# State space input projection of a two-block layer as seven half-size products instead of eight, with three VectorE sums placed later

## The chip, the cores and the metric

The kernel runs on one core of one Trainium2 chip. The metric is the device time of one execution in microseconds (us), as the median of several runs. All data are float32. A core has a matrix engine (TensorE, PE in the profile, whose weight loads are listed as PEld), VectorE (DVE), ScalarE (ACT), GpSimd (POOL), and a queue engine (SyncE, SP) that issues most of the transfers from memory.

## The reference

256 tokens of width 1024 go through two blocks. The first is a hybrid of latent attention, gated linear attention and memory attention with a feed-forward part. The second is a state space branch beside dilated attention. The change touches the first projection of the second block, and the order of three sums elsewhere. Cut to that:

```
h = rms_norm_2(x, norm_w)
proj = h @ w_in                                # 256 x 1024 times 1024 x IN_WIDTH
u_s, z_s, q, k, v, z_a, r_s, r_a = split(proj) # u_s: 1024 columns
y_s = s5_branch(u_s, ...)                      # B u, a scan over time of 64 x 64 complex states, C h + D u,
                                               # gelu, glu
q = partial_rope(rms_norm_2(q)); k = partial_rope(rms_norm_2(k))
y_a = dilated_attention(q, k, v)
m = sigmoid(r_s) * (y_s * silu(z_s)) @ w_ssm_out + sigmoid(r_a) * (y_a * silu(z_a)) @ w_attn_out
x = x + m @ w_o
```

## The kernel before

The whole layer is one program without loops on the device. Each engine has its own instruction stream, in the order in which the source writes it, and semaphores join them. Nothing is reordered by a scheduler: what an engine has queued behind a wait waits with it.

Weights come through `ring`, three slots of 2 MB. SP issues the loads in the order of `JOBS` and waits before each (L512) until the job that used the slot last is finished. The two PSUM pairs of 1024 columns serve alternate outputs (`OUTS`), and an output may start only when the output two places ahead of it is taken out of its pair. Two `turned` banks hold transposes (and the state space outputs), two `score` banks hold scores (and the inputs of the states).

Most 1024 x 1024 projections are already "groups" (`group_multiply`, from L2073): rows and weights are cut in halves, and seven products of half the size in each dimension stand for eight. VectorE makes the sums of rows (`group_rows`: S1 to S4), the sums of weights (`group_t1` to `group_t4`), and puts the results together (`group_z`, `group_v`, `group_c12`, `group_c22`, `group_last`); ScalarE copies the products Q1 and Q5 out of PSUM (`group_copy`) and takes out the first block (`group_first`). Product 5 needs T1 and S1, 7 needs T3 and S3, 3 needs S4, 6 needs T2, 4 needs T4 and Z. T2 may only be made when product 5 is done, for both lie in one buffer.

The state space inputs `us0` and `us1` are not a group before the change. They are plain jobs, each by halves of tokens: `us0` on the first 128 tokens, the transposes of the second 128 tokens (`turn_rows("x", xn3, 1)`), then `us1` on the first tokens, and both on the second tokens. ScalarE takes them to `uT` (L844), and `stacks` copies `uT` to `u2`, half by VectorE (L1766, semaphore `u2_ready`) and half by ScalarE (L850).

Then the state space stage runs, eight rounds of m. In each TensorE makes `drive(m)` (the inputs of the states, L2479) and `states(m - 1)` (their outputs, L2460 to L2468), and fills the time with quarters of the jobs of `early`: dv0, dv1, dv2, zs0, zs1, za, dq0, dq1 (`fill`; a quarter is four matmuls of 512 columns, or eight of 256). VectorE scans the states and adds each output tile to `uT` (`ssm_out`). After `states(7)` VectorE runs `ssm_out(7)`, the argument of the gelu (`gelu_z`), and `dqk(0)`, the norm and rotation of the first queries. TensorE may turn those (`turn_dqk(0)`, L1987) only when `dqk(0)` is done (semaphore `dqk_rows`). Behind that it has the job dq2 and then `turn_dqk(1)`, which waits for `dqk(1)` in the same way.

Two other places matter. In the stage of memory attention, group `MV` (values of the memory) is followed by group `GT` (a gate), and a loop of i from 0 to 8 mixes them with scores and with levels of gated linear attention. In the dilated attention, a loop over s runs group `RA` between the scores.

Of the kernel before, what the change touches and what calls it, by code (L numbers as in the profile page):

```python
# [12 lines left out]
P = 128  # L13
# [70 lines left out]
DK = UP + 4  # L84
# [5 lines left out]
def jobs_table():  # L90
# [20 lines left out]
    j = [(f"us{i}", "w_in_2", C_US + 512 * i, 512) for i in range(2)]  # L111
    j += [(f"dv{g}", "w_in_2", C_DVV + DW * g, DW) for g in range(NDIL)]
# [17 lines left out]
ORDERS[GT] = ORDERS[UP] = ORDERS[WP] = (1, 2, 5, 7, 3, 6, 4)  # L130
# [3 lines left out]
ROWS = (0, 1, 1, 2, 3, 4) + 4 * (5,) + (6, 6, 6, 7, 8, 9)  # L134
# [4 lines left out]
BY_TOKENS = (("gate2", "gate3"), ("wo0", "wo1"), ("us0", "us1"))  # L139
HALVES = []  # L140
for _job in JOBS:
# [12 lines left out]
SPLIT_TOKENS = ("us0", "us1")  # L154
CHANNEL_MAJOR = {"ga", "us0", "us1", "zs0", "zs1", "za"}
# [49 lines left out]
    "u_ready": "state space inputs, even and odd steps stacked", "u2_ready": "first half of those stacks",  # L205
# [29 lines left out]
def act_at(i, n):  # L235

    return 3 * i + n - max(i - SO, 0) - (i > GT)
# [12 lines left out]
def build(nc, d, out):  # L250
    with ExitStack() as ctx:
# [133 lines left out]
        tail_t2 = {DK: arena[:, 0:2048], RS: arena[:, 2048:4096], RA: rows_raw, GLU: rows_raw, SO: arena[:, work_at:work_at + 2048], WP: arena[:, work_at + 4096:work_at + 6144]}  # L385
        tail_rows = {DK: m_tok, RS: m_tok, RA: m_tok, GLU: zs, SO: arena[:, work_at + 2048:work_at + 4096], WP: rows_raw}

# [24 lines left out]
        def group(i):  # L412
# [3 lines left out]
            w = [ring[:, STREAMED.index(JOB[f"g{i}{x}"]) % RING, :].rearrange("p (k n) -> p k n", n=DM) for x in "xy"]  # L416
            b11, b12, b21, b22 = (x[:, :, 512 * n:512 * n + 512] for x in w for n in range(2))
            if i < DK:
# [12 lines left out]
        def temporaries(i):  # L431
            if i >= DK:
                return tail_q1, tail_q5, tail_q5, tail_q1
            if i == MV:
                return copied_q1, across, across, copied_q1
            if i == GT:
# [34 lines left out]
        def _(sp):  # L471
# [21 lines left out]
            for n, j in enumerate(STREAMED):  # L493
# [9 lines left out]
                if n >= RING:  # L503

                    before = JOBS[STREAMED[n - RING]][0]
                    if before[:-1] in GROUPS:
# [59 lines left out]
        def _(act):  # L566
# [12 lines left out]
            def take(name, dst, func=ACT.Copy, scale=1.0, cols=512):  # L579

                for t in range(TT):
                    p = arrived(name, 1 if name in SPLIT_TOKENS else t)
# [54 lines left out]
            def group_first(i, dst, scale=1.0):  # L637
# [5 lines left out]
                act.activation(dst, src, ACT.Relu if UP <= i < DK else ACT.Copy, scale=scale).then_inc(sem("group_act"), 1)  # L643
# [197 lines left out]
            for i in range(2):  # L841
                for t in range(TT):
                    p = arrived(f"us{i}")
                    ins = act.activation(uT[:, 1024 * i + 512 * t:1024 * i + 512 * t + 512], p[:, 512 * t:512 * t + 512], ACT.Copy)  # L844
# [99 lines left out]
        def _(dve):  # L944
# [83 lines left out]
            def group_t1(i):  # L1028

                _, _, (b11, b12, _, _), _, (t2, _) = group(i)  # L1030
                weights_in(f"g{i}x")
                if i == GT:
# [305 lines left out]
            group_rows(GT)  # L1338
# [48 lines left out]
            group_middle(MV, vm4[1], vm4[3])  # L1387
            level_diff(0)
            gt4 = by_tokens(gate_buf)
            h, (_, _, z, v), biased = group(GT)[0], temporaries(GT), ckv[:, 0:512]  # L1390
            for i in range(9):
                if i == 0:
                    group_t1(GT)
                if i == 1:
# [70 lines left out]
                if i in (4, 6):  # L1465
                    gate_gain((i - 4) // 2)
# [256 lines left out]
            turns_real(64, high)  # L1723
            turns_imag(64, high)

# [123 lines left out]
            for s in range(DH // 2 + 1):  # L1849
                if s == 2:  # L1850
                    group_c12(RA, ra4[1])
                if s < DH // 2:
# [6 lines left out]
                    if s == 0:  # L1859
                        group_t3(RA)  # L1860
# [108 lines left out]
        def _(pe):  # L1969
# [25 lines left out]
            def matmuls(name, half):  # L1995
# [17 lines left out]
                if o in SPLIT_TOKENS:  # L2013
                    return [(p[:, SEQ * c + P * half:SEQ * c + P * half + P], ws[:, k, P * c:P * c + P],
                             act_(k)[:, P * half:P * half + P], k == 0, k == nk - 1) for c in range(4) for k in range(nk)]
# [10 lines left out]
            def half_job(name, half, sub=0, of=1):  # L2026
# [3 lines left out]
                if half == 0 and sub == 0:  # L2030
# [4 lines left out]
                    if i >= 2 and FIRST_JOB[o] == name:  # L2035
# [37 lines left out]
            def group_multiply(i, q, channels=False, sub=0, of=1):  # L2073
# [18 lines left out]
                bank_, rows, weights = {1: (1, a11, b11), 5: (3, s1, t2), 2: (1, a12, b21), 7: (4, s3, t3), 3: (3, s4, b22),  # L2092
# [7 lines left out]
                elif q == 5:  # L2100
                    summed(1)
                    rows_summed(1)
                elif q == 2:
# [15 lines left out]
                onto = q in (2, 3, 4)  # L2119
# [368 lines left out]
            pe.wait_ge(sem("ca_ready"), 2)  # L2488
            for m in range(8):
# [185 lines left out]
```

## Time and profile before

| | |
|---|---|
| median of 3 runs | 966.28 us (965.92 to 966.91) |
| the profiled execution's own time | 964.69 us |
| its span in the profile | 962.8 us |
| TensorE busy | 947.7 us, 98% |
| VectorE busy | 719.3 us, 75% |
| ScalarE busy | 224.1 us, 23% |
| chain that ended last, by engine | PE 89%, DVE 8%, ACT 2% |
| share of 16 DMA engines, queue of the weights | 39.8% |

TensorE is busy nearly always, so the time is its work plus its few waits. A float32 matmul of the source stands as two MATMUL records in the trace, so "x64" there is 32 matmuls. The mean duration of a record is longer than the distance between two starts, because matmuls are pipelined: the pace is read from the start of one group of records to the start of the next. The 1.9 us between the span and the execution's own time lie outside the program.

### The profile page before, as it was taken

Reading aid. Unit: us, or ns where it says so; the run is one execution under the profiler, and the core shown is the slowest. Engines: PE = TensorE matmul, PEld = TensorE weight load, DVE = VectorE, ACT = ScalarE, POOL = GpSimd, SP = SyncE. Lnnn points to the kernel's source line nnn. Section 1 sums busy time; section 2 is a strip of 40 time slices with the busy share of each in tenths; the row PEclk is TensorE's granted clock in tenths of the full one; section 3 lists DMA queues with packets and bytes.
Section 4 is the critical chain, followed back from the end, with each engine's and each line's share of the span. In section 5 each row is a group of like instructions: output and inputs, shape, how many; then the busy total and the mean of one; then the engine's idle time right before and its main releaser. Section 6 shows DMA issues by size and latency. Waiting matters only on the chain.

```text
span 962.8 us, 12510 instructions
## 1 busy us (share of the span) xinstructions
PE 947.7 (98%) x4998; PEld 587.7 (61%) x4998; DVE 719.3 (75%) x1260; ACT 224.1 (23%) x442; POOL 23.3 (2%) x27
## 2 busy tenths in 40 slices
PE   7999999999999999999999999999999999999998
PEld 6944445754555449999844459447854444468544
DVE  4875964578968887966899863988968689674667
ACT  4313412223231223422200011201012221434100
POOL 0100000000002500000000000000000000000000
PEclk9999999999999999999999999999999999999999
DMA  9551731434534524344444433523424443321631
GB/s 329 151 197 43 285 131 44 175 117 147 165 120 124 174 107 167 131 176 175 175 175 174 174 122 142 175 88 113 151 88 175 161 143 142 113 97 45 223 127 45
DMA packets 51770, 139.76 MB, mean 145 GB/s; under 512 B 3968, under 2 KB 7904, under 8 KB 51712
## 3 DMA queue, kind: packets, MB, share of 16 engines
q1 hardware_dynamic: 50256, 135.07, 39.8%
q0 software_dynamic: 1248, 3.80, 1.6%
q8 instruction: 40, 0.66, 0.3%
q14 instruction: 18, 0.15, 0.0%
q10 hardware_dynamic: 208, 0.08, 0.0%
HBM read 137.90 MB, written 1.05 MB: 144 GB/s over the span
## 4 chain that ended last, share of the span: by engine, by line
PE 89%; DVE 8%; ACT 2%; issue 1%; DMA 1%; DVEq 0%; ACTq 0%
PE pair L2042 30%; PE pair L2127 22%; PE pair L2123 16%; PE pair L2384 6%; DVE arena L974 4%; PE turned L1987 4%; PE score L2384 3%; PE turned L2384 1%; PE score L2479 1%; PE score L2551 1%; PE score L2564 1%; PE score L2226 1%; PE score L2225 1%; PE score L2281 1%; DMA ident<-in_c_ident 1%
## 5 line engine op out<-in xcount | busy, mean ns | idle before, releaser
L2042 PE MATMUL pair<-ring,hT 128*128 128x512 f32 (+2 forms) x512 | 213.6, 572 | 0.9 <-ACT hT L622 0.9
L974 DVE TENSOR_TENSOR arena<-arena 128x256 f32<-128x256 f32 (+6 forms) x332 | 196.7, 607 | 17.2 <-PE score L2384 4.0
L2042 PEld LDWEIGHTS pair<-ring,hT 128*128 128x128 f32 x512 | 95.3, 190 | 102.6 <-issue 97.7
L2127 PE MATMUL pair<-ring,arena 128*128 128x512 f32 x192 | 85.8, 594 | 0.0
L2127 PE MATMUL pair<-ring,hT 128*128 128x512 f32 x184 | 84.0, 598 | 1.3 <-DMA ring<-in_w_in 0.7
L2127 PE MATMUL pair<-arena 128*128 128x512 f32 x176 | 79.8, 595 | 0.4 <-DVE arena L974 0.4
L974 DVE TENSOR_TENSOR arena<-pair,arena 128x512 f32<-128x512 f32 x60 | 41.5, 692 | 49.6 <-PE pair L2127 25.6
L2042 PE MATMUL pair<-hT,ring 128*128 128x128 f32 (+2 forms) x464 | 76.2, 324 | 0.2 <-ACT hT L622 0.2
L974 DVE TENSOR_TENSOR arena<-ring 128x2048 f32<-128x2048 f32 (+1 forms) x39 | 72.3, 1855 | 2.5 <-DMA ring<-in_w_ssm_out 1.2
L2042 PEld LDWEIGHTS pair<-hT,ring 128*128 128x128 f32 (+1 forms) x464 | 66.0, 188 | 8.6 <-ACT hT L622 1.0
L2123 PE MATMUL pair<-arena 128*128 128x128 f32 x544 | 64.0, 276 | 0.0
L2123 PEld LDWEIGHTS pair<-arena 128*128 128x128 f32 x544 | 62.2, 192 | 0.3 <-issue 0.2
L2127 PEld LDWEIGHTS pair<-ring,arena 128*128 128x128 f32 x192 | 35.6, 190 | 41.4 <-issue 41.3
L2127 PEld LDWEIGHTS pair<-ring,hT 128*128 128x128 f32 x184 | 33.4, 190 | 39.5 <-issue 38.4
L2127 PEld LDWEIGHTS pair<-arena 128*128 128x128 f32 x176 | 32.8, 190 | 39.3 <-issue 38.4
L2123 PE MATMUL pair<-hT,ring 128*128 128x128 f32 x480 | 55.7, 275 | 0.0
L2123 PEld LDWEIGHTS pair<-hT,ring 128*128 128x128 f32 x480 | 54.7, 192 | 0.7 <-issue 0.5
L1987 PEld LDWEIGHTS turned<-ident,arena 128*128 128x128 f32 (+1 forms) x363 | 41.1, 141 | 22.7 <-issue 16.5
L593 ACT ACTIVATE arena<-turned 128x512 f32<-128x512 f32 (+2 forms) x66 | 32.8, 540 | 87.5 <-PE turned L1987 87.5
L1987 PE MATMUL turned<-ident,arena 128*128 128x128 f32 (+1 forms) x363 | 49.9, 275 | 2.2 <-DVE arena L1876 0.9
L974 DVE TENSOR_TENSOR arena<-arena,ring 128x2048 f32<-128x2048 f32 (+1 forms) x24 | 46.5, 1937 | 1.7 <-PE pair L2123 0.6
L2384 PE MATMUL pair<-ring,arena 128*128 128x512 f32 x96 | 43.5, 592 | 0.0
(226 smaller groups left out, 1009.3 us busy)
## 6 DMA issues: line engine op xcount, KB each, us to landing
ring<-in_w_in SPq DMA_DIRECT2D x33, 2048.0 KB, 8.4
ring<-in_w_up SPq DMA_DIRECT2D x8, 2048.0 KB, 8.6
ring<-in_w_down SPq DMA_DIRECT2D x8, 2048.0 KB, 7.9
ring<-in_w_o SPq DMA_DIRECT2D x4, 2048.0 KB, 8.0
ring<-in_w_mem_kv SPq DMA_DIRECT2D x2, 2048.0 KB, 7.7
ring<-in_w_glu SPq DMA_DIRECT2D x2, 2048.0 KB, 8.1
ring<-in_w_ssm_out SPq DMA_DIRECT2D x2, 2048.0 KB, 7.8
ring<-in_w_ukv SPq DMA_DIRECT2D x4, 512.0 KB, 3.7
```

Of the source, the lines that this page charges most:

```text
L593: act.activation(dst, src, ACT.Copy).then_inc(sem("turned_taken"), 1)
L974: return dve.tensor_tensor(o, a, b, op)
L1987: ins = pe.transpose(b[0:x.shape[1], a:a + rows], x, ident[0:rows, 0:rows])
L2042: ins = pe.matmul(o_, s, m, start=a, stop=b)
L2123: ins = pe.matmul(h[bank_][:, P * c:P * c + P], weights[:, k, P * c:P * c + P], rows[:, k, :], start=not onto and c == 0 and k == 0, stop= ...
L2127: ins = pe.matmul(h[bank_], rows[:, k, :], weights[:, k, :], start=not onto and k == 0, stop=k == 3, skip_group_check=True)
L2225: pe.matmul(o, qnT[:, SEQ * h + P * t:SEQ * h + P * t + P], knT[:, SEQ * h:SEQ * h + w], start=True, stop=False)
L2226: ins = pe.matmul(o, qpT[r, SEQ * (h // 2) + P * t:SEQ * (h // 2) + P * t + P], kpeT[r, 0:w], start=False, stop=True)
L2281: ins = pe.matmul(b[:, SEQ * t:SEQ * t + SEQ], s[:, 256 * t + P * k:256 * t + P * k + P], vm3[:, k, EV * h:EV * h + EV], start=k == 0, sto ...
L2384: ins = pe.matmul(product[q], rows[:, k, :], weights[:, k, :], start=g == 0 and k == 0, stop=g == 7 and k == 1, skip_group_check=True)
L2479: ins = pe.matmul(b[:, 256 * h + P * i:256 * h + P * i + P], bt[r, 2048 * i + P * n:2048 * i + P * n + P], u2[r, CH * n:CH * n + CH], star ...
L2551: ins = pe.matmul(b[:, cols], qdT[r, a + P * t:a + P * t + P], kdT[r, a:a + w], start=True, stop=True)
```

## The change

`us0` and `us1` become the group `US`, number 10, and the groups behind it move up by one. Its weights are split by columns and not by rows: the first load holds columns 512 to 1023 of all 1024 rows, so products 1 and 2 need that load alone. Product 2 has a PSUM bank of its own (half 2 of the second pair) and is added to Q1 by VectorE. Products 1 and 2 take the place of `us0` on the first tokens; after the transposes comes the first half of `dv0`, which had been in `early`, and then products 5, 7, 3, 6, 4. `early` starts three quarters later, and each round takes its quarters from three places on. VectorE makes the sums in its stream around `turns_real` and `turns_imag(64, high)`. ScalarE copies Q1 and Q5 instead of four blocks.

Apart from it, `group_rows(GT)` moves behind `group_middle(MV, ...)`, the two `gate_gain` move from the ends of i = 4 and 6 to the starts of i = 4 and 5, `group_t3(RA)` moves behind the first heads of s = 0, and `group_t4(RA)` from s = 0 to s = 1.

```diff
-    j = [(f"us{i}", "w_in_2", C_US + 512 * i, 512) for i in range(2)]
-    j += [(f"dv{g}", "w_in_2", C_DVV + DW * g, DW) for g in range(NDIL)]
+    out += [(f"g{US}{'xy'[i]}", f"g{US}{'ab'[i]}", "w_in_2", 0, DM, C_US + 512 * (1 - i), 512) for i in range(2)]
+    j = [(f"dv{g}", "w_in_2", C_DVV + DW * g, DW) for g in range(NDIL)]
...
+                    if before[:-1] == f"g{US}":
+                        sp.wait_ge(sem("group_product"), product_at(US, 4 if before[-1] == "x" else 6))
...
-            for i in range(2):
-                for t in range(TT):
-                    p = arrived(f"us{i}")
-                    ins = act.activation(uT[...], p[:, 512 * t:512 * t + 512], ACT.Copy)
-                    if t == 0:
-                        ins.then_inc(sem("u_ready"), 1)
-                ins.then_inc(sem("taken_act"), 1)
-            act.wait_ge(sem("taken_act"), taken("us1")[1])
+            group_copy(US, 1)
+            group_copy(US, 5)
+            act.wait_ge(sem("last_out"), US + 1)
             for h, jj, s, src, dst in stacks(1):
...
-            group_rows(GT)
...
             group_middle(MV, vm4[1], vm4[3])
+            group_rows(GT)
             level_diff(0)
...
+                if i in (4, 5):
+                    gate_gain(i - 4)
...
-                if i in (4, 6):
-                    gate_gain((i - 4) // 2)
...
             turns_real(64, high)
+            group_t1(US)
+            dve.wait_ge(sem("turned_taken"), T_B + 4)
+            group_rows(US)
+            us4 = by_channels(uT)
+            h, (q1, _, _, v) = group(US)[0], temporaries(US)
+            dve.wait_ge(sem("group_product"), product_at(US, 2))
+            dve.wait_ge(sem("group_act"), act_at(US, 1))
+            link(tt(us4[1], blocks(h[2], us4[1]), blocks(q1, us4[1]), ALU.add))
+            group_t3(US)
             turns_imag(64, high)
+            group_t2(US)
+            group_t4(US)
+            group_z(US)
+            group_v(US)
+            dve.wait_ge(sem("group_product"), product_at(US, 3))
+            mark(tt(us4[0], blocks(h[3], us4[0]), blocks(v, us4[0]), ALU.add), "first_out")
+            group_c22(US, us4[2])
...
-            dve.wait_ge(sem("taken_act"), taken("us0")[1])
             for h, jj, s, src, dst in stacks(0):
...
+            group_last(US, us4[3])
...
-                    if s == 0:
-                        group_t3(RA)
...
                 if s == 0:
+                    group_t3(RA)
                     group_t2(RA)
+                if s == 1:
                     group_t4(RA)
-                if s == 1:
...
-            half_job("us0", 0)
+            group_multiply(US, 1, True)
+            group_multiply(US, 2, True)
             pe.wait_ge(sem("x_rows"), 6)
             turn_rows("x", xn3, 1)
-            half_job("us1", 0)
+            pe.wait_ge(sem("group_act"), act_at(US, 1))
+            half_job("dv0", 0, own_wait=True)
             is_turned("x")
-            half_job("us0", 1)
-            half_job("us1", 1)
+            for q in (5, 7, 3, 6, 4):
+                group_multiply(US, q, True)
+            pe.wait_ge(sem("first_out"), US + 1)
...
+            fill(early, 2, 1)
             for m in range(8):
...
                 drive(m)
-                fill(early, 3 * m, 1)
-                fill(early, 3 * m + 1, 1)
+                fill(early, 3 * m + 3, 1)
+                fill(early, 3 * m + 4, 1)
                 if m:
                     states(m - 1)
-                fill(early, 3 * m + 2, 1)
-            fill(early, 12, 2)
+                fill(early, 3 * m + 5, 1)
+            fill(early, 27, 1)
+            fill(early, 28, 1)
             states(7)
-            fill(early, 13, 2)
-            fill(early, 14, 2)
+            fill(early, 29, 1)
             fill(early, 15, 2)
```

The order on TensorE around the projection, before: the first rows are the end of the feed-forward's last products and the transposes of the first tokens; `pair<-hT,ring` is `us0` and `us1`, `pair<-ring,hT` is dv0, `score<-arena` is `drive`.

```order
L2384 MATMUL score<-arena 128x512 x2
L2042 MATMUL pair<-hT,ring 128x128 x32
L1987 MATMUL turned<-ident,arena 128x128 x8
L2042 MATMUL pair<-hT,ring 128x128 x96
L2479 MATMUL score<-arena 128x128 x8
L2042 MATMUL pair<-ring,hT 128x512 x12
```

The same place of the changed kernel: products 1 and 2, the transposes, half of dv0, products 5, 7 and 3, 6, 4, and a quarter of dv0.

```order
L2403 MATMUL score<-arena 128x512 x2
L2142 MATMUL pair<-hT,ring 128x128 x32
L2006 MATMUL turned<-ident,arena 128x128 x8
L2058 MATMUL pair<-ring,hT 128x512 x8
L2142 MATMUL pair<-arena 128x128 x16
L2142 MATMUL pair<-arena,ring 128x128 x32
L2142 MATMUL pair<-arena 128x128 x16
L2142 MATMUL pair<-hT,ring 128x128 x16
L2058 MATMUL pair<-ring,hT 128x512 x4
L2501 MATMUL score<-arena 128x128 x8
```

128 matmuls of 128 columns have become 112, and 12 of the 512-column matmuls now stand ahead of the first `drive`.

TensorE at the end of the state space stage, before: the last `drive`, quarters of dq0, `states(6)`, more of dq0, `states(7)` (the second set of `turned<-arena`), the rest of dq0 and dq1, then `turn_dqk(0)` (`turned<-ident,arena`) and the job dq2.

```order
L2466 MATMUL turned<-arena 32x128 x8
L2460 MATMUL turned<-arena 32x128 x4
L2468 MATMUL turned<-arena 32x127 x8
L2042 MATMUL pair<-ring,hT 128x512 x24
L1987 MATMUL turned<-ident,arena 128x128 x8
L2042 MATMUL pair<-ring,hT 128x512 x16
```

The same place of the changed kernel.

```order
L2488 MATMUL turned<-arena 32x128 x8
L2482 MATMUL turned<-arena 32x128 x4
L2490 MATMUL turned<-arena 32x127 x8
L2058 MATMUL pair<-ring,hT 128x512 x12
L2006 MATMUL turned<-ident,arena 128x128 x8
L2058 MATMUL pair<-ring,hT 128x512 x16
```

Between the last state outputs and the transposes of the queries stand 12 matmuls of 512 columns instead of 24.

## Rows read from the trace of the kernel before

**Rows 1.** The page: TensorE's busy time, and its granted clock in 40 slices.
```profile
PE 947.7 (98%) x4998; PEld 587.7 (61%) x4998; DVE 719.3 (75%) x1260; ACT 224.1 (23%) x442; POOL 23.3 (2%) x27
...
PEclk9999999999999999999999999999999999999999
```

**Rows 2.** Timeline of TensorE, projection: start, us, engine, line, operation, records [idle before].
```profile
571.28 7.41 PE L2042 MATMUL pair<-hT,ring 128*128 128x128 f32 x64 [0.17 <-ACT hT L622]
578.53 1.04 PE L1987 MATMUL turned<-ident,arena 128*128 128x128 f32 x8
579.40 21.60 PE L2042 MATMUL pair<-hT,ring 128*128 128x128 f32 x192
600.93 1.16 PE L2479 MATMUL score<-arena 64*128 64x128 f32 x16
602.03 10.57 PE L2042 MATMUL pair<-ring,hT 128*128 128x512 f32 x24
```

**Rows 3.** Timeline of ScalarE, same place.
```profile
579.23 2.17 ACT L622 ACTIVATE hT<-turned,pcol 128x128 f32<-128x128 f32 x8 [6.13 <-PE turned L1987]
...
609.20 0.60 ACT L583 ACTIVATE arena<-pair 128x512 f32<-128x512 f32 x1 [1.62 <-PE pair L2042]
```

**Rows 4.** Loads by SP's line 512, from 568 to 572 us: issues, and time to landing.
```profile
L512 SPq DMA_DIRECT2D ring<-in_w_in x2: 368/368/368, 568.5 to 571.1; - x2
...
DMA to landing us min/median/max: 8.3/9.6/11.0
```

**Rows 5.** The same from 100 to 104 us.
```profile
L512 SPq DMA_DIRECT2D ring<-in_w_in x2: 368/368/368, 100.1 to 103.5; - x2
...
DMA to landing us min/median/max: 8.4/9.8/11.1
```

**Rows 6.** Timeline of VectorE, projection.
```profile
576.12 7.28 DVE L974 TENSOR_TENSOR arena<-arena 128x1024 f32<-128x1024 f32 x6
595.08 3.57 DVE L1766 COPY arena<-arena 32x512 f32<-32x512 f32 x8 [11.69 <-ACT arena L844]
```

**Rows 7.** Timeline of VectorE, end of the state space stage and first queries.
```profile
714.37 0.48 DVE L1774 SCALAR_TENSOR_TENSOR arena<-arena,pcol,turned 128x256 f32<-128x256 f32 x1 [5.02 <-PE turned L2468]
...
723.58 1.22 DVE L1737 TENSOR_REDUCE stats<-arena 128x16 f32<-128x1024 f32 x1 [2.24 <-ACT arena L886]
...
730.58 0.62 DVE L974 TENSOR_TENSOR arena<-arena 128x128 f32<-128x128 f32 x2
731.24 1.42 DVE L974 TENSOR_TENSOR arena<-hT 128x512 f32<-128x512 f32 x2
...
734.14 5.00 DVE L974 TENSOR_TENSOR arena<-arena 128x1024 f32<-128x1024 f32 x4
...
746.84 2.29 DVE L974 TENSOR_TENSOR arena<-ring 128x2048 f32<-128x2048 f32 x1
```

**Rows 8.** Timeline of TensorE, same place.
```profile
714.16 20.87 PE L2042 MATMUL pair<-ring,hT 128*128 128x512 f32 x48
734.87 1.04 PE L1987 MATMUL turned<-ident,arena 128*128 128x128 f32 x8
...
749.48 1.04 PE L1987 MATMUL turned<-ident,arena 128*128 128x128 f32 x8
```

**Rows 9.** Timeline of TensorE, first product of group GT.
```profile
224.69 3.67 PE L2127 MATMUL pair<-ring,hT 128*128 128x512 f32 x8 [0.58 <-DVE arena L974]
```

**Rows 10.** Timelines of VectorE and then TensorE, end of the loop over i.
```profile
293.28 1.23 DVE L974 TENSOR_TENSOR arena<-arena,gains 128x1024 f32<-128x1024 f32 x1
...
300.26 1.56 PE L2308 MATMUL score<-arena 128*128 128x256 f32 x6 [0.82 <-DVE arena L1425]
```

**Rows 11.** Timeline of TensorE, dilated attention.
```profile
826.76 0.87 PE L1987 MATMUL turned<-ident,arena 128*128 128x128 f32 x6 [0.92 <-DVE arena L1876]
...
835.77 0.70 PE L2551 MATMUL score<-arena 64*128 64x256 f32 x4 [0.41 <-DVE stats L1254]
```

**Rows 12.** Timeline of TensorE, its first matmuls.
```profile
5.63 3.96 PE L2134 MATMUL score<-ident 128*128 128x128 f32 x20 [5.63 <-DMA ident<-in_c_ident]
```

More of the change, by code:

```diff
@@ L83 @@
 RG, MV, GT, UP = 3, 4, 5, 6
-DK = UP + 4
+US = UP + 4
+DK = US + 1
 RS = DK + 1
@@ L129 @@
 ORDERS = {i: (1, 5, 2, 7, 3, 6, 4) for i in range(NG)}
-ORDERS[GT] = ORDERS[UP] = ORDERS[WP] = (1, 2, 5, 7, 3, 6, 4)
+ORDERS[GT] = ORDERS[US] = ORDERS[UP] = ORDERS[WP] = (1, 2, 5, 7, 3, 6, 4)
 ORDERS[RA] = (1, 5, 2, 7, 6, 3, 4)
-ROWS = (0, 1, 1, 2, 3, 4) + 4 * (5,) + (6, 6, 6, 7, 8, 9)
+ROWS = (0, 1, 1, 2, 3, 4) + 4 * (5,) + (6, 7, 7, 7, 8, 9, 10)
 LAST_JOB = {job[1]: job[0] for job in JOBS}
 FIRST_JOB = {job[1]: job[0] for job in reversed(JOBS)}
-BY_TOKENS = (("gate2", "gate3"), ("wo0", "wo1"), ("us0", "us1"))
+BY_TOKENS = (("gate2", "gate3"), ("wo0", "wo1"))
 HALVES = []
@@ L152 @@
 BY_DVE = {"gg", "wo0", "wo1", "ao0", "ao1"} | {f"gate{i}" for i in range(2, 6)}
-SPLIT_TOKENS = ("us0", "us1")
-CHANNEL_MAJOR = {"ga", "us0", "us1", "zs0", "zs1", "za"}
+CHANNEL_MAJOR = {"ga", "zs0", "zs1", "za"}
 STREAMED = [n for n, job in enumerate(JOBS) if job[2]]
@@ L204 @@
     "m0_ready": "TensorE: B times C, by group", "m0_taken": "that product out of PSUM",
-    "u_ready": "state space inputs, even and odd steps stacked", "u2_ready": "first half of those stacks",
+    "u2_ready": "first half of those stacks",
     "u2_late": "ScalarE: their second half",
@@ L415, in group @@
             h = {1: a[:, 0:512], 3: a[:, 512:1024], 2: b[:, 0:512], 4: b[:, 512:1024]}
-            w = [ring[:, STREAMED.index(JOB[f"g{i}{x}"]) % RING, :].rearrange("p (k n) -> p k n", n=DM) for x in "xy"]
-            b11, b12, b21, b22 = (x[:, :, 512 * n:512 * n + 512] for x in w for n in range(2))
-            if i < DK:
+            w = [ring[:, STREAMED.index(JOB[f"g{i}{x}"]) % RING, :].rearrange("p (k n) -> p k n", n=512 if i == US else DM) for x in "xy"]
+            if i == US:
+                b11, b12, b21, b22 = (x[:, 4 * n:4 * n + 4, :] for n in range(2) for x in w)
+            else:
+                b11, b12, b21, b22 = (x[:, :, 512 * n:512 * n + 512] for x in w for n in range(2))
+            if i < US:
                 t2, t3 = (x.rearrange("p (k n) -> p k n", n=512) for x in ((sum_t2[i], sum_t3) if i < UP else (up_t2, up_t3)))
@@ L505, in _ @@
                     before = JOBS[STREAMED[n - RING]][0]
-                    if before[:-1] in GROUPS:
+                    if before[:-1] == f"g{US}":
+                        sp.wait_ge(sem("group_product"), product_at(US, 4 if before[-1] == "x" else 6))
+                    elif before[:-1] in GROUPS:
                         sp.wait_ge(sem("group_product"), product_at(GROUPS.index(before[:-1]), 7 if before[-1] == "x" else 4))
@@ L1031, in group_t1 @@
                 weights_in(f"g{i}x")
+                if i == US:
+                    weights_in(f"g{i}y")
                 if i == GT:
@@ L2024, in _, with half_job @@
             finished = [0]
-            def half_job(name, half, sub=0, of=1):
+            def half_job(name, half, sub=0, of=1, own_wait=False):
                 j = JOB[name]
@@ L2034, in half_job @@
                     i = OUTS.index(o)
-                    if i >= 2 and FIRST_JOB[o] == name:
+                    if i >= 2 and FIRST_JOB[o] == name and not own_wait:
                         by, v = taken(OUTS[i - 2])
@@ L2090, in free @@
                     pe.wait_ge(sem(by), v)
-                bank_, rows, weights = {1: (1, a11, b11), 5: (3, s1, t2), 2: (1, a12, b21), 7: (4, s3, t3), 3: (3, s4, b22),
+                bank_, rows, weights = {1: (1, a11, b11), 5: (3, s1, t2), 2: (2 if i == US else 1, a12, b21), 7: (4, s3, t3), 3: (3, s4, b22),
                                         6: (2, s2, t2), 4: (4, a22, b21)}[q]
@@ L2100, in group_multiply @@
                 elif q == 5:
+                    came(f"g{i}{'y' if i == US else 'x'}")
                     summed(1)
                     rows_summed(1)
+                elif q == 2 and i == US:
+                    free(OUTS[b - 2])
                 elif q == 2:
@@ L2118, in group_multiply @@
                     pe.wait_ge(sem("group_z"), i + 1)
-                onto = q in (2, 3, 4)
+                onto = q in (3, 4) or q == 2 and i != US
                 if channels:
```

16 lines of the change are left out of this document (7 added, 9 removed).

## The prediction

> **What bounds the kernel now.** I read the page first: TensorE is busy 98% of the span at the full granted clock in all 40 slices [rows 1]. So the time is TensorE's stream, and an edit counts only by the work that it takes out of that stream and by the waits that it opens or closes there. VectorE has a quarter of its time free, but its order decides when TensorE may go on. Next I read the timelines of TensorE, ScalarE, VectorE and the loads around the projection, and then followed TensorE's stream to the places at which it meets VectorE again.
>
> In the projection TensorE has no wait after 571.28 [rows 2]: from there it runs 163.59 us without one, up to the first queries' transposes at 734.87 [rows 2, 8]. VectorE meanwhile stands still for 11.69 us ahead of its copies [rows 6]. The other waits of TensorE that the change can reach are 0.58 [rows 9], 0.82 [rows 10], 0.92 and 0.41 [rows 11].
>
> **The work saved.** 192 records take 600.93 - 579.40 = 21.53 us, 0.112 each and 0.224 for a matmul of the source [rows 2]. The group has 7 x 16 = 112 of them where there were 128: 16 x 0.224 = **-3.6 us**.
>
> **First wait: Q1 has to be copied.** Products 1 and 2 take as long as `us0` on the first tokens, so the transposes start at 578.53 as before and end their issue at 579.40 [rows 2]. Then stood `us1`, which could run while ScalarE took the transposes out. Now TensorE waits for `group_copy(US, 1)`, because dv0 goes into the bank of Q1. ScalarE has the copy queued behind eight evictions that wait for the very transposes: 579.23 + 2.17 = 581.40, and a copy of 512 columns takes 0.60 [rows 3], so 582.05. The weights of dv0 are issued at 571.1 and land 11.0 later, at 582.1 [rows 4], the same moment. Cost: 582.1 - 579.4 = **+2.7 us** (bounds 2.5 and 3.0). That half of dv0 does not come free: it fills the time of VectorE's sums, but begins only behind this wait.
>
> **The sums, hidden.** `turns_real` ends half way in 7.28 us, at 579.8 [rows 6]. A sum of weights takes 2.29, four sums of rows 734.14 - 731.24 = 2.9 [rows 7]. T1 is ready at 582.1, the rows at 585.0, us4[1] at 585.7, T3 at 588.0, `turns_imag` at 591.7. TensorE's half of dv0 (eight matmuls; 48 records in 20.71 us are 0.863 for each matmul [rows 8]) ends at 589.1, so products 5 and 7 find their sums. Product 5 ends at 592.7, T2 at 595.2, T4 at 597.6, both ahead of products 6 (599.9) and 4 (603.5). `first_out` comes at 605.2, ahead of TensorE's 607.1. The copies of 3.57 us [rows 6] make `u2_ready` at 609.5; TensorE has a quarter of dv0 until 610.6. The 15 us that VectorE has to add lie in the time in which it stood still; this cover has 1.1 us left, and beyond that each us would be TensorE's.
>
> **A load that starts later.** dv1 uses the slot of the group's first load, and SP waits for product 4, so it is issued at 607.2, behind all of the group. A load takes 8.3 to 8.4 when one follows closely, for the second waits and not the first (8.3 beside 11.0, 8.4 beside 11.1) [rows 4, 5]. So dv1 lands at 615.6. TensorE wants it after `drive(0)` (1.1 [rows 2]) and one quarter (3.5), at 615.1. Cost: **+0.5 us** (bounds 0, and 5 if two loads issued 0.4 us apart shared the rate from the start; the trace's closest neighbours are 2.7 us apart, and I take the lower price).
>
> **Second wait: the first queries come too late.** This is the term that decides. `drive(0)` starts 3 quarters later in the job list, so every round of the state space stage stands 10.4 us deeper in TensorE's work, `states(7)` too. Behind it were 24 matmuls, 20.71 us [rows 8]; now 12, 10.4 us. What VectorE must do between `states(7)` and `turn_dqk(0)` is unchanged, and it is a chain: it starts at 714.37, waiting 5.02 for the output [rows 7]; `ssm_out(7)` and the gelu's argument end at 723.58 - 2.24 = 721.34; `dqk(0)` runs from 723.58 to 731.20 [rows 7]. Without the 2.24 us of waiting for dq0, which is now complete earlier, the chain is 6.97 + 0.04 + 7.62 = 14.6 us, and 14.9 from the moment 0.2 ahead at which TensorE leaves `states(7)`, wake-up included. TensorE had 20.7 us to hide it in and keeps 10.4: 14.9 - 10.4 = **+4.5 us** of waiting at the transposes (bounds 4.0 and 5.0).
>
> **The second queries.** From the end of `dqk(0)` to that of `dqk(1)` VectorE needs 746.8 - 731.2 = 15.6 us [rows 7]; TensorE needs 749.48 - 734.87 = 14.6 between the two transposes [rows 8]. VectorE was 749.48 - 746.8 = 2.7 us ahead; after the second wait both start together, so **+1.0 us** more. For the third, `dqk(2)` starts as soon as dq2 is squared, 7.6 us of chain beside 14.6 us of TensorE: it has room, and the stream is back in its old order.
>
> **The three sums.** `group_rows(GT)`, 2.9 us, stood ahead of the block for which the 0.58 us wait was [rows 9]; behind the change VectorE starts that block as soon as MV's product 6 is there. The wait goes; but VectorE itself gets on no earlier, and TensorE meets it again later in the loop: **-0.4 us** (bounds -0.6 and 0). `gate_gain`, 1.23 us, stood ahead of the level whose later copies hold TensorE 0.82 us [rows 10]; at the starts of i = 4 and 5 VectorE is idle. Part of it was hidden by the wait for a score: **-0.4 us** (bounds -0.8 and 0). `group_t3(RA)` and `group_t4(RA)`, 2.29 each [rows 7], leave the ways to the 0.92 and the 0.41 us wait [rows 11]: some 0.9 us at first. But T4 now lies in s = 1 ahead of `group_t1(GLU)`, and pushes VectorE's first scores of s = 2 back by about 1.1 us, where TensorE waits for both score banks. I take **0** (bounds -0.9 and +0.4), for the delay is as long as the gain.
>
> **The sum.** -3.6 + 2.7 + 0.5 + 4.5 + 1.0 - 0.4 - 0.4 + 0 = +4.3 us. The profiled execution took 964.69 us, 1.9 more than its span, and would take 969.0; the median of the runs is 1.6 above it, 966.28, and becomes **970.6 us**. The lead of half a projection costs more at its end than the eighth product gives.
>
> **Rivals.** (a) Not slower: the queries' chain still fits. It decides at the point where TensorE's work behind `states(7)` reaches 14.9 us; if the outputs came a quarter and more earlier, or the gelu's argument ran ahead, 5.5 us of the sum go and 970.6 becomes 965.1. For it: VectorE waits 5.02 us for those outputs, so it could start earlier if TensorE gave them. Against: TensorE's order is fixed, and 12 matmuls stand there. Chance 0.12.
> (b) The full gain: neither the copy of Q1 nor the queries stop TensorE; -3.6 and about -1 from the sums, 961.7. It needs two of my chains wrong, so 0.05.
> (c) A slower clock after the longest wait. No stretch of the trace shows less than the full clock, 2.4 GHz, in its slices [rows 1], but after the 5.63 us in which TensorE stood still at the start its first 20 records took 3.96 us, 0.198 each [rows 12], against 0.112 later [rows 2]: 1.7 us for such a start. A wait of 4.5 us is nearly as long. 1.0 us of it would vanish in the wait for the second queries, so 971.3; after both waits 973. Chance 0.15. The Trainium skill, "TensorE: Matmul & The Clock Gate", section "Why this matters for your kernels", says that idle gaps between bursts of matmuls bring the engine back to half its clock; by that the dearer end of this rival would hold, and only the slow first records speak for it here.
> (d) The two loads share the rate, dv1 lands 4 to 5 us later: 975. Against it is the pattern of rows 4 and 5. Chance 0.05.
>
> **How the numbers follow.** The forecast itself has 0.63; 970.6 with its own bounds of 969.3 to 972. The range reaches down past the bounds of the small terms and toward (a), and up over (c): 967.0 to 973.4. About 0.2% (1.9 us) is what a measurement of this kernel can tell from no change. Slower by more: the forecast, (c), (d) and a slip of the terms, 0.82. Within: (a), 0.11. Faster by more: (b) and part of (a), 0.07.
>
> **What would show each step.** In the changed profile TensorE's busy time falls by about 3.6 us and its idle time rises by about 8. One idle of some 2.5 us stands ahead of dv0's first matmul, put down to ScalarE's copy or the load; one of some 4.4 ahead of the first queries' transposes and one of 1 ahead of the second, both put down to VectorE's rotation; one of up to 0.5 at dv1's first quarter. VectorE no longer waits 2.24 us for the squares of dq0. The 0.58 us at GT is gone. If the transposes of the queries show no wait, the central term is wrong; if `drive(0)` waits for VectorE's copies, the cover of the sums was thinner than I reckoned; if the matmuls behind the long wait run at 0.2 us a record, it is (c).

## The result: half a per cent slower, and the profile after

The changed kernel takes 971.12 us (970.37 to 972.92, 4 runs) where the kernel before takes 966.47 us: a ratio of 1.0055, 95% interval 1.0043 to 1.0067. The quotient of the two medians is 1.0048, inside that interval, so the loss is 4.7 to 5.3 us. Run again later the changed kernel took 970.84 us, 1.0055 (1.0043 to 1.0068). The forecast was 970.6 us. One execution of the first experiment below (1406.62 us, mean granted clock 0.655) and one of the second (1230.17 us, 0.754) are in the medians given there, but not in the ratios.

The page after, as its first lines and its granted clock:

```profile
span 968.4 us, 12476 instructions
...
PE 947.7 (98%) x4966; PEld 585.6 (60%) x4966; DVE 735.3 (76%) x1274; ACT 223.5 (23%) x440; POOL 23.4 (2%) x27
...
PEclk9999999999999999999999999999999999999999
```

The span is 5.6 us longer. TensorE has 32 records fewer than in [rows 1] (16 matmuls of the source) and yet the same busy time, 947.7 us. That is a first sign that some of its records have become slower. VectorE has 16 us more work, the sums of the new group.

The timeline of TensorE in the projection, which answers to [rows 2]:

```profile
569.98 7.41 PE L2142 MATMUL pair<-hT,ring 128*128 128x128 f32 x64 [0.17 <-ACT hT L629]
577.23 1.04 PE L2006 MATMUL turned<-ident,arena 128*128 128x128 f32 x8
580.73 8.80 PE L2058 MATMUL pair<-ring,hT 128*128 128x512 f32 x16 [2.47 <-ACT arena L642]
589.37 3.73 PE L2142 MATMUL pair<-arena 128*128 128x128 f32 x32
...
610.76 1.16 PE L2501 MATMUL score<-arena 64*128 64x128 f32 x16
```

Products 1 and 2 take the place of `us0`. Then TensorE stands idle for 2.47 us until ScalarE's line 642, the copy of Q1, is done. The half of dv0 behind it takes 589.37 - 580.73 = 8.64 us, where 8 matmuls at 0.863 would be 6.90. From there all products follow without a wait: the sums are hidden.

ScalarE and the two loads at the same place, as in [rows 3, 4]:

```profile
577.92 2.18 ACT L629 ACTIVATE hT<-turned,pcol 128x128 f32<-128x128 f32 x8 [6.13 <-PE turned L2006]
579.94 0.65 ACT L642 ACTIVATE arena<-pair 128x512 f32<-128x512 f32 x1
...
L519 SPq DMA_DIRECT2D ring<-in_w_in x2: 368/368/368, 567.2 to 569.8; - x2
...
DMA to landing us min/median/max: 8.1/9.4/10.8
```

The copy ends at 580.6, and the load of dv0's weights lands at 569.8 + 10.8 = 580.6.

The two loads behind the group, dv1's first, with the shortest and the longest time to landing. Asked for alone, the one issued at 607.4 lands after 7.9 us:

```profile
L519 SPq DMA_DIRECT2D ring<-in_w_in x2: 368/476/583, 607.4 to 607.8; - x2
...
DMA to landing us min/median/max: 7.9/10.4/12.9
```

TensorE at the end of the state space stage, as in [rows 8], and VectorE, as in [rows 7]:

```profile
724.10 10.57 PE L2058 MATMUL pair<-ring,hT 128*128 128x512 f32 x24
739.05 1.94 PE L2006 MATMUL turned<-ident,arena 128*128 128x128 f32 x8 [4.38 <-issue]
740.78 14.51 PE L2058 MATMUL pair<-ring,hT 128*128 128x512 f32 x32
755.12 1.04 PE L2006 MATMUL turned<-ident,arena 128*128 128x128 f32 x8
...
724.31 0.48 DVE L1794 SCALAR_TENSOR_TENSOR arena<-arena,pcol,turned 128x256 f32<-128x256 f32 x1 [7.32 <-PE turned L2490]
...
731.32 1.22 DVE L1757 TENSOR_REDUCE stats<-arena 128x16 f32<-128x1024 f32 x1
...
738.32 0.62 DVE L976 TENSOR_TENSOR arena<-arena 128x128 f32<-128x128 f32 x2
...
753.93 0.62 DVE L976 TENSOR_TENSOR arena<-arena 128x128 f32<-128x128 f32 x2
```

VectorE begins behind `states(7)` at 724.31 and ends the rotation of the first queries at 738.94. TensorE is through with its 12 matmuls at 734.5 and starts the transposes at 739.05. The profile names no releaser for those 4.38 us ("issue"); the end of the rotation 0.1 us ahead of them does. A label is no proof, so the runs below test it.

Behind both waits the granted clock fell. The stretches of the changed kernel (columns: stretch, its length, then busy us and records of PE, PEld, DVE, ACT, POOL, then the granted clock as a share of 2.4 GHz, the share of the DMA engines, GB/s):

```profile
575.00:580.00 5.00, 3.26 (x30) 3.02 (x28) 4.93 (x4) 2.08 (x9) 0.00 (x0) 1.00 0.98 364
580.00:585.00 5.00, 4.27 (x6) 1.82 (x7) 4.80 (x7) 0.59 (x2) 0.00 (x0) 0.66 0.02 6
...
735.00:740.00 5.00, 0.95 (x5) 0.98 (x6) 4.79 (x10) 1.77 (x4) 0.00 (x0) 0.86 0.84 296
740.00:745.00 5.00, 5.00 (x14) 2.77 (x13) 4.83 (x6) 1.20 (x2) 0.00 (x0) 0.80 0.31 125
```

A share of 0.66 or 0.80 over 5 us is a part of that time at the lower level, 1.2 GHz. Read in steps of 1 us, the clock is still at its full level when TensorE works again behind the first wait (1.00 from 580 to 581), and at 0.50 from 582 to 584. At the second it falls while TensorE still stands idle (0.79 from 738 to 739) and is at 0.50 from 739 to 742. The forty slices of the page are too coarse to show it.

Where the 5.6 us lie, from TensorE's marks in the two traces (each step is the distance between two starts, after less before; the three quarters of dv0 that stand elsewhere are counted out at 10.36 us):

| stretch of TensorE | after less before, us |
|---|---|
| start to the end of the last transposes of MV (216.44 for 217.07) | -0.63; the wait for the first load was 4.9 for 5.63 us |
| to the projection (569.98 for 571.28) | -0.67 |
| to the first `drive` (40.78 - 10.36 for 29.65) | +0.77 = -3.6 + 2.6 + 1.7 |
| to the end of `states(7)` (113.34 for 113.23) | +0.11 |
| to the first queries' transposes (14.95 for 20.71 - 10.36) | +4.60 |
| to the second queries' transposes (16.07 for 14.61) | +1.46 |
| to the end of the span | -0.04 |
| sum | +5.60 |

### The profile page after: what moved, and what is told of

It reads as the page before. It is cut to its first block, busy times and chain, and to the rows that moved or that the text cites. A ratio compares the mean times of both kernels' runs of the same rounds, so it can differ in the third digit from the quotient of the medians.

```text
span 968.4 us, 12476 instructions
## 1 busy us (share of the span) xinstructions
PE 947.7 (98%) x4966; PEld 585.6 (60%) x4966; DVE 735.3 (76%) x1274; ACT 223.5 (23%) x440; POOL 23.4 (2%) x27
## 4 chain that ended last, share of the span: by engine, by line
PE 86%; DVE 10%; ACT 2%; issue 1%; DMA 0%; DVEq 0%; ACTq 0%
PE pair L2058 28%; PE pair L2146 20%; PE pair L2142 18%; DVE arena L976 6%; PE pair L2403 6%; PE turned L2006 3%; PE score L2403 3%; PE turned L2403 1%; PE score L2574 1%; PE score L2501 1%; PE score L2245 1%; DVE ring L976 1%; PE score L2244 1%; PE score L2587 1%; ACT hT L629 1%
## 5 line engine op out<-in xcount | busy, mean ns | idle before, releaser
L2058 PE MATMUL pair<-ring,hT 128*128 128x512 f32 (+2 forms) x512 | 216.3, 577 | 3.3 <-ACT arena L642 2.5
L976 DVE TENSOR_TENSOR arena<-arena 128x256 f32<-128x256 f32 (+6 forms) x333 | 197.4, 607 | 14.9 <-PE score L2403 4.1
L976 DVE TENSOR_TENSOR arena<-pair,arena 128x512 f32<-128x512 f32 x64 | 44.3, 692 | 55.3 <-PE pair L2146 25.8
L2146 PE MATMUL pair<-ring,arena 128*128 128x512 f32 x192 | 85.8, 594 | 0.0
L2142 PE MATMUL pair<-arena 128*128 128x128 f32 x608 | 71.5, 275 | 0.0
L2142 PEld LDWEIGHTS pair<-arena 128*128 128x128 f32 x608 | 69.6, 192 | 0.7 <-issue 0.7
L2142 PE MATMUL pair<-hT,ring 128*128 128x128 f32 x576 | 66.8, 275 | 0.2 <-ACT hT L629 0.2
L2142 PEld LDWEIGHTS pair<-hT,ring 128*128 128x128 f32 x576 | 65.6, 192 | 1.7 <-ACT hT L629 1.0
L2146 PEld LDWEIGHTS pair<-arena 128*128 128x128 f32 x176 | 32.8, 190 | 39.3 <-issue 38.4
L2058 PE MATMUL pair<-hT,ring 128*128 128x256 f32 (+1 forms) x208 | 47.2, 383 | 0.0
L2142 PE MATMUL pair<-arena,ring 128*128 128x128 f32 x384 | 46.0, 277 | 0.0
L2142 PEld LDWEIGHTS pair<-arena,ring 128*128 128x128 f32 x384 | 44.0, 192 | 1.3 <-issue 1.0
```

Of the source, the lines that this page charges most:

```text
L976: return dve.tensor_tensor(o, a, b, op)
L2058: ins = pe.matmul(o_, s, m, start=a, stop=b)
L2142: ins = pe.matmul(h[bank_][:, P * c:P * c + P], weights[:, k, P * c:P * c + P], rows[:, k, :], start=not onto and c == 0 and k == 0, stop= ...
L2146: ins = pe.matmul(h[bank_], rows[:, k, :], weights[:, k, :], start=not onto and k == 0, stop=k == 3, skip_group_check=True)
```

## Experiments

**The state outputs earlier.** If VectorE's chain behind `states(7)` is what TensorE waits for, giving it five quarters to hide in and not three has to remove both waits at the queries.

```diff
-            fill(early, 27, 1)
-            fill(early, 28, 1)
             states(7)
+            fill(early, 27, 1)
+            fill(early, 28, 1)
             fill(early, 29, 1)
```

> The changed kernel with one edit: states(7) stands directly behind the last round, so that 20 matmuls of 512 columns (17.3 us) and not 12 (10.4 us) lie between the last state outputs and the first queries' transposes. Theory (VectorE's chain of 14.9 us behind states(7) is what TensorE waits for): the waits of 4.4 us and of about 1 us ahead of the first and second queries go, and with them the slow clock behind the first of them; 971.1 - 4.6 - 1.5 = 965.0 us. Rival (ScalarE's squares or evictions, or the TensorE stream itself, set those transposes): the wait stays, 970 to 971 us. Second rival: states(7) now waits for VectorE's scan of round 7, which ends only some 0.4 us ahead of it; then a new wait of up to 1 us stands there, 966 us.

Measured: 965.22 us, 0.9993 of the kernel before (0.9984 to 1.0002), so 6.0 us below the changed kernel. TensorE at that place:

```profile
714.89 0.65 PE L2488 MATMUL turned<-arena 128*32 128x128 f32 x16
...
716.40 17.43 PE L2058 MATMUL pair<-ring,hT 128*128 128x512 f32 x40
733.67 1.04 PE L2006 MATMUL turned<-ident,arena 128*128 128x128 f32 x8
734.54 13.90 PE L2058 MATMUL pair<-ring,hT 128*128 128x512 f32 x32
748.28 1.04 PE L2006 MATMUL turned<-ident,arena 128*128 128x128 f32 x8
```

No wait stands there any more, and no slow transposes. `states(7)` itself does not wait for the scan. The position of the last outputs in TensorE's stream alone made the loss at the queries. It is the main one: mended, the change is level with the kernel before. The first wait is still there, 2.39 us long.

**The copy first.** The first wait has two ends that coincide, the copy and the load. Taking one away tells whether the other holds.

```diff
             for t in range(TT):
                 act.wait_ge(sem("residual"), 2 * TT + 2 * t + 2)
                 row_norm(t, xres[:, t, :], 0, "x", uT[:, 0:1024])
+                if t == 1:
+                    group_copy(US, 1)
                 turned_rows(t, hT, "norm_w_2")
-            group_copy(US, 1)
             group_copy(US, 5)
```

> The changed kernel with one edit: ScalarE copies Q1 ahead of the eight evictions of the second tokens' transposes. Theory (the copy and the load of dv0's weights end at the same moment, 580.6 us): TensorE waits as long as before, now for the load; 970.9 us, gain at most 0.2 us. Rival (only the copy holds TensorE): the wait of 2.5 us and the slow clock behind it go, 967.0 us.

Measured: 971.27 us, 1.0053 (1.0040 to 1.0066): no gain. ScalarE's copy and TensorE's first dv0 record:

```profile
574.60 0.60 ACT L642 ACTIVATE arena<-pair 128x512 f32<-128x512 f32 x1 [2.11 <-issue]
...
581.61 8.80 PE L2059 MATMUL pair<-ring,hT 128*128 128x512 f32 x16 [2.65 <-DMA ring<-in_w_in]
```

The copy is done at 575.2, more than 6 us earlier relative to the work around it, and TensorE waits 2.65 us all the same, now for the load. An edit at ScalarE alone, where the profile's releaser pointed, gains nothing. (The profiled execution, 974.38 us, was the longest of the five in the ratio.) The load alone holds TensorE; whether the copy alone would hold it as long was not run.

**Kept busy.** Is the slow clock caused by TensorE's own idling, and what does it cost? Extra matmuls fill the waits without shortening them.

```diff
+            pe.wait_ge(sem("residual"), 8)
+            for _n in range(10):
+                pe.matmul(bank["score"][0][:, 0:P], ident[:, :], ident[:, :], start=True, stop=True)
             pe.wait_ge(sem("group_act"), act_at(US, 1))
             half_job("dv0", 0, own_wait=True)
...
+            pe.wait_ge(sem("score_taken"), n_unit["score"])
+            for _n in range(18):
+                pe.matmul(bank["score"][0][:, 0:P], ident[:, :], ident[:, :], start=True, stop=True)
             pe.wait_ge(sem("ssm_taken"), 8)
```

> The changed kernel with matmuls of the identity in the two long waits (10 of 128 columns ahead of dv0, 18 ahead of the first queries' transposes), written to a score bank that nobody reads then. They are extra work and do not shorten the waits. Theory (the slow stretches behind the waits, 1.7 us at dv0 and 1.5 us at the queries of which about 1 would be waited out anyway, come from TensorE's idling): 971.1 - 1.7 - 0.5 = 968.9 us, and the granted clock stays at its full level. Rival (the slow stretches have nothing to do with the idling): 971.1 us or a little more.

Measured: 968.82 us, 1.0036 (1.0024 to 1.0048), 1.9 thousandths or 1.8 us below the changed kernel, with more work in it.

```profile
581.09 7.11 PE L2058 MATMUL pair<-ring,hT 128*128 128x512 f32 x16 [0.44 <-DMA ring<-in_w_in]
...
733.25 4.18 PE L2540 MATMUL score<-ident 128*128 128x128 f32 x36
737.79 1.06 PE L2006 MATMUL turned<-ident,arena 128*128 128x128 f32 x8 [0.36 <-issue]
...
753.34 1.09 PE L2006 MATMUL turned<-ident,arena 128*128 128x128 f32 x8 [0.75 <-DVE arena L976]
...
735.00:740.00 5.00, 4.64 (x34) 3.76 (x34) 4.76 (x11) 1.60 (x4) 0.00 (x0) 1.00 1.00 396
```

The granted clock stays at its full level, with a mean of 1.000 in each of the five executions, where all nine executions of the changed kernel had 0.996. The half of dv0 takes 7.1 us again and the transposes 1.06 where they took 1.94. The wait for the second queries, which the slow clock had covered in the changed kernel, comes to light: 0.75 us of idle, 737.79 to 753.34 being 15.55 where 14.61 is the work alone.

**The three sums alone**, on the kernel before (the projection is left as it was; the edit is that of the change, at GT, the gains and RA).

> The kernel before with the three moved sums alone (rows of GT, the two gains, T3 and T4 of RA); the projection stays as it was. Theory: GT's wait goes and the one at the end of the loop is halved, RA gives 0.9 us and takes it back; -0.7 us, 965.8 us. Rival (the dilated attention's gain is real and only the state space part costs): -1.6 us, 964.9 us. Rival on the other side: a wait for VectorE elsewhere takes it all back, 966.5 us.

Measured: 964.50 us, 0.9989 (0.9981 to 0.9998), 1.0 us faster, with an interval that nearly reaches 1. It holds both the -0.7 us of the theory and the -1.6 us of the first rival; only the trace tells them apart. TensorE:

```profile
224.41 3.60 PE L2126 MATMUL pair<-ring,hT 128*128 128x512 f32 x8
...
250.50 0.70 PE L2296 MATMUL score<-arena 128*32 128x32 f32 x32 [0.51 <-DVE stats L1254]
...
300.08 1.56 PE L2307 MATMUL score<-arena 128*128 128x256 f32 x6 [0.45 <-DVE arena L1427]
...
826.12 0.87 PE L1986 MATMUL turned<-ident,arena 128*128 128x128 f32 x6 [0.45 <-DVE arena L1874]
...
853.29 0.70 PE L2550 MATMUL score<-arena 64*128 64x256 f32 x4 [0.85 <-DVE stats L1254]
```

GT's wait of [rows 9] is gone, but a new one of 0.51 us stands 26 us later: TensorE, ahead now, meets VectorE's scores. The wait of [rows 10] is halved. In the dilated attention both waits of [rows 11] shrink, 0.92 to 0.45 and 0.41 to nothing, and 0.85 us come back in the scores of s = 2, as the theory had it.

**Without the lead.** The lead undone: no dv0 in the projection, the rounds and the place of `states(7)` as before.

```diff
-            pe.wait_ge(sem("group_act"), act_at(US, 1))
-            half_job("dv0", 0, own_wait=True)
             is_turned("x")
...
-            fill(early, 2, 1)
...
-                fill(early, 3 * m + 3, 1)
-                fill(early, 3 * m + 4, 1)
+                fill(early, 3 * m, 1)
+                fill(early, 3 * m + 1, 1)
...
-                fill(early, 3 * m + 5, 1)
-            fill(early, 27, 1)
-            fill(early, 28, 1)
+                fill(early, 3 * m + 2, 1)
+            fill(early, 12, 2)
             states(7)
-            fill(early, 29, 1)
+            fill(early, 13, 2)
+            fill(early, 14, 2)
```

> The changed kernel without the lead: no half of dv0 between the transposes and product 5, no quarter of it ahead of the first drive, and the quarters of the rounds and the place of states(7) as in the kernel before. Theory: TensorE now waits for VectorE's sums, about 3.5 us ahead of product 5, 1.6 ahead of product 7 and 2.3 ahead of the first drive, while 24 matmuls hide the queries' chain again. Against the kernel before +3.9 us in the projection (the saved 3.6 included) and -0.7 from the three sums: 969.7 us, up to 971 with a slow clock. Rival (the sums are ready anyway and the lead was not needed): 962 us. Rival (the queries' wait does not come from the lead): 974 us or more.

Measured: 969.35 us, 1.0041 (1.0027 to 1.0055), 3.4 us over the kernel before.

```profile
582.33 5.44 PE L2142 MATMUL pair<-arena 128*128 128x128 f32 x32 [3.36 <-DVE arena L976]
...
604.68 1.16 PE L2499 MATMUL score<-arena 64*128 64x128 f32 x16 [2.62 <-DVE arena L1785]
...
717.91 20.87 PE L2058 MATMUL pair<-ring,hT 128*128 128x512 f32 x48
738.62 1.04 PE L2006 MATMUL turned<-ident,arena 128*128 128x128 f32 x8
```

Now TensorE waits for the sums, 3.36 us ahead of product 5 and 2.62 ahead of the first `drive`, and the wait of 1.6 us that I expected ahead of product 7 vanished, because product 5 ran slowly (5.27 us for 3.57) in the meantime. At the queries there is no wait. So the lead does what it is for, and the lead is what opens the wait 130 us later. Neither with it nor without it does the group pay in this form.

**Both mended.** The two waits attacked at once, by order alone.

```diff
             group_multiply(US, 1, True)
-            group_multiply(US, 2, True)
+            group_multiply(US, 2, True, 0, 2)
             pe.wait_ge(sem("x_rows"), 6)
             turn_rows("x", xn3, 1)
+            group_multiply(US, 2, True, 1, 2)
+            is_turned("x")
+            group_multiply(US, 5, True)
             pe.wait_ge(sem("group_act"), act_at(US, 1))
             half_job("dv0", 0, own_wait=True)
-            is_turned("x")
-            for q in (5, 7, 3, 6, 4):
+            for q in (7, 3, 6, 4):
...
-            turns_real(64, high)
             group_t1(US)
...
             group_t3(US)
+            turns_real(64, high)
             turns_imag(64, high)
```

with ScalarE's copy as in the second experiment and `states(7)` as in the first.

> The changed kernel with both waits attacked. ScalarE copies Q1 ahead of the evictions; the transposes stand in the middle of product 2; product 5 stands ahead of dv0's half and covers the rest of its load; VectorE makes T1, the rows, us4[1] and T3 ahead of turns_real; states(7) stands behind the last round. Theory: about 1.1 us of waiting is left ahead of product 5, too short for a slow clock, so -3.3 us in the projection and -6.1 us at the queries: 961.9 us, below both kernels. Rival (the sums now come late for products 7, 6 or the first drive, whose cover was 1.2 us): 963 to 965 us.

Measured: 962.74 us, 0.9969 (0.9958 to 0.9980), and 962.19 us, 0.9966 (0.9952 to 0.9979) when it was run again: 3.2 us faster than the kernel before.

> The kernel of e6 again, as the measure for e7 on the same chip: 0.9969 of the kernel before.

```profile
580.85 3.81 PE L2144 MATMUL pair<-arena 128*128 128x128 f32 x32 [0.93 <-DVE arena L978]
584.49 7.03 PE L2060 MATMUL pair<-ring,hT 128*128 128x512 f32 x16
...
609.18 1.16 PE L2505 MATMUL score<-arena 64*128 64x128 f32 x16
```

A wait of 0.93 us is left, for S1, and the clock stays up. Products 7 and 6 and the first `drive` do not wait, so the rival's late sums are not there. The two places gave what was expected of them: from the projection to the first `drive` TensorE takes 37.55 us for 40.78 (-3.2), and from the end of `states(7)` to the second queries 31.88 us for 31.02, with 8 matmuls more in it, 6.9 us (-6.0). The profiled execution lost 1.65 us ahead of the projection (571.63 for 569.98), where the edit changes nothing.

**T1 of GLU later.** The last 0.85 us.

```diff
                     group_c22(RA, ra4[3])
-                    group_t1(GLU)
...
+                    if s == 2:
+                        group_t1(GLU)
                     for e in range(2):
                         h = 2 * s + e
```

> The kernel of e6 with one edit more: T1 of GLU (2.29 us on VectorE) moves from s = 1 into the idle time of VectorE between the second and the third scores of s = 2. Theory (T4 of RA and T1 of GLU together push VectorE's first scores of s = 2 back, and TensorE waits 0.85 us for the score banks): that wait goes and the 0.9 us gained earlier stay; 0.85 us below e6 on the same chip, 0.9991 of it. Rival (the third scores, now up to 0.5 us later, pass their delay on to the transposes, whose room was 1.9 us): no gain.

Measured: 961.09 us, 0.9954 (0.9941 to 0.9966), beside 0.9966 of the kernel without this edit on the same chip: 1.1 us less, a difference that the two intervals by themselves do not separate. The trace shows its place: the scores that waited 0.85 us follow at once. From the matmuls ahead of them to the end of the span it takes 111.41 us, beside 112.08 in the trace of the kernel without the edit: by the traces 0.67 of the 1.1 us are its doing.

```profile
847.39 1.98 PE L2149 MATMUL pair<-ring,hT 128*128 128x512 f32 x4
849.30 0.70 PE L2579 MATMUL score<-arena 64*128 64x256 f32 x4
```

This is the fastest version, 4.9 us below the kernel before.

**The changed kernel again.**

> The changed kernel itself, on the chip of e6 and e7: 1.0055 of the kernel before. If the slow clock behind its two waits does not come in every execution, its runs spread over some 3 us and wider than the kernel before's; if it is always there, they spread as those do.

Measured: 970.84 us (970.46 to 971.52, 5 runs). Its stretches, columns as above:

```profile
580.00:585.00 5.00, 3.56 (x9) 1.68 (x10) 4.83 (x6) 1.35 (x5) 0.00 (x0) 1.00 0.12 40
...
735.00:740.00 5.00, 1.98 (x9) 2.01 (x10) 4.76 (x11) 1.35 (x4) 0.00 (x0) 0.65 0.95 373
740.00:745.00 5.00, 5.00 (x9) 1.98 (x9) 4.83 (x6) 0.59 (x1) 0.00 (x0) 0.67 0.09 37
```

TensorE in the same trace, at the half of dv0 and at the transposes of the first and second queries:

```profile
581.44 7.10 PE L2058 MATMUL pair<-ring,hT 128*128 128x512 f32 x16 [2.41 <-ACT arena L642]
...
738.02 1.94 PE L2006 MATMUL turned<-ident,arena 128*128 128x128 f32 x8 [4.37 <-issue]
...
755.27 1.04 PE L2006 MATMUL turned<-ident,arena 128*128 128x128 f32 x8
```

In this execution the clock did not fall behind the first wait. Behind the second it was low for longer: 0.65 and 0.67 for 0.86 and 0.80, and the second transposes follow after 755.27 - 738.02 = 17.25 us, not 16.07. So 1.7 us were saved at one place and 1.2 paid at the other. That fits the five times, which lie within 1.1 us where the expectation had some 3 us. The mean granted clock, which is known of every execution, tells how often it falls: 0.996 in all nine of the changed kernel, and never under 0.999 in the 43 of the kernel before that stand beside the experiments. In the first experiment, where only the first wait is left, it is 0.998 in five of the ten executions in the ratio and 1.000 in the other five. Why it falls behind that wait in some executions and not in others stays open.

## Why the prediction was right, point by point

The time (971.12 for 970.6), the sign and the main mechanism came out as forecast, by these steps.

- *The work saved*, 3.6 us: right. It is hard to see in the page, because slowed records filled TensorE's busy time up again; my own sign for it, a busy time lower by 3.6 us, did not appear, and the idle time rose by 5.6 us and not by 8.
- *First wait*, 2.7 us: 2.63 by the starts. That copy and load end together was right: both are at 580.6 in the trace, and in the second experiment, the copy gone, the wait stays at 2.65.
- *The sums, hidden*: right, at every product. The first `drive` found its copies made 1.1 us ahead (VectorE ended them at 609.66, TensorE came at 610.76).
- *The later load*, +0.5: 0.11. The first of two loads issued 0.4 us apart landed in 7.9 us, not 8.4, while the second took 12.9. Rival (d), sharing, was wrong.
- *Second wait*, 4.5 us: 4.60. The chain took 14.95 us where 14.9 had been worked out. The first experiment confirmed its cause.
- *Second queries*, 1.0: 1.46 in the changed kernel, 0.94 with TensorE kept busy. The rest is the slow clock.
- *The three sums*, -0.8: -0.67 up to the projection and nothing in the dilated attention; -1.0 us when measured alone. The give-back at s = 2 was named beforehand and stands in the trace.
- *The slow clock*, rival (c): it was there in every execution, though its chance was put at 0.15. It cost 1.7 us behind the first wait in the profiled execution and 0.5 net behind the second; in the profile of the kernel run again it cost nothing behind the first and 1.7 net behind the second. Kept busy, the kernel gains 1.8 us. The central sum had it at nothing. This is the one step that was mis-sized, and the median of 971.12 us lies nearer to this rival's 971.3 than to the forecast. My evidence for it was weak: the slow first records [rows 12] ran at a granted clock of 1.00 by the profile (5 to 10 us). The price behind both waits, 973 us, I had also put down to the Trainium skill, "TensorE: Matmul & The Clock Gate", section "Why this matters for your kernels". Its advice there is against idle gaps longer than the first wait, so it speaks for the second wait alone.

That the total is nearer than its parts is partly luck: the slow clock (about +2) was missed, the load came 0.4 cheaper, and the span of the profiled execution (5.6 us longer) includes a start that was 0.6 us quicker than before. By the medians the difference is 4.7 us, by the forecast 4.3. The profiled execution of the kernel before (964.69 us) lies 1.8 us below its median, that of the changed kernel (970.37) 0.8 below, and this spread takes another 1.0 us off the difference.

## What to carry to other kernels

When work is pulled ahead to cover one stage, look at what it used to cover where it came from: a fixed order of jobs is a budget, and here the 10.4 us given to the projection were missing behind the last state outputs, where a chain of 14.9 us on another engine had been hidden. Where a releaser is named, ask what else ends at that moment; removing the named one alone gained nothing. And on an engine that is busy all the time, a wait of some us costs more than its length, for the matmuls behind it may run at half the clock.

## What the runs showed of the hardware

- TensorE's granted clock fell to 1.2 GHz behind idle times of 2.47, 2.65 and 3.36 us in three profiled executions, and in the course of all three of 4.4 us. It did not behind 2.39 us in another, behind 2.41 us when the changed kernel was profiled again, nor behind 2.62 us (the first `drive` without the lead). It stayed up behind 0.93 us. The low stretch cost 1.7 us each time at dv0 or product 5. The Trainium skill, "TensorE: Matmul & The Clock Gate", section "Why this matters for your kernels", advises against long idle gaps between bursts of matmuls. The rows agree at 4.4 us, and show a low clock at some gaps of 2.5 us too.
- Extra matmuls of the identity in the two waits kept the clock up in all five executions and made the kernel 1.8 us faster with more work.
- Two loads of 2 MB issued 0.4 us apart on one queue landed after 7.9 and 12.9 us, at 615.3 and 620.7. Two issued 2.6 us apart landed after 8.1 and 10.8 us. The first was not held up by the second; the second was longer on its way.
